# Delta rounds of a two-block model: solve steps one in a slot, spreads in two GpSimd operations, doubling levels four and five moved by five slots

## The reference

```python
k_beta = kc * bc[..., None]
v_beta = vc * bc[..., None]
lower = jnp.where(strict, jnp.einsum('bhnik,bhnjk->bhnij', k_beta, kc) * decay, 0.0)
t_inv = lax.linalg.triangular_solve(eye + lower, eye, left_side=True, lower=True, unit_diagonal=True)
u = t_inv @ v_beta
w = t_inv @ (k_beta * jnp.exp(gc)[..., None])
intra = jnp.where(tril, jnp.einsum('bhnik,bhnjk->bhnij', qc, kc) * decay, 0.0)
def step(state, xs):
    v_new = u_i - w_i @ state
    o_i = qd_i @ state + intra_i @ v_new
    state = state * jnp.exp(gl_i)[..., None, None] + jnp.swapaxes(ks_i, -1, -2) @ v_new
```

## Time and profile before

| | us |
|---|---|
| median of 3 runs | 3521.67 |
| lowest, highest | 3516.02, 3525.56 |
| the profiled execution | 3509.0 |
| its span | 3507.2 |

### The profile page before, as it was taken

The page is one execution under the profiler, slowest core; times in us unless marked ns, Lnnn a source line. Parts: engine busy times, 40 slices in busy tenths (PEclk is TensorE's granted clock), DMA queues, the critical chain, the costliest instruction groups (busy, mean ns, idle before and its releaser), DMA issues.

```text
span 3507.2 us, 51167 instructions
## 1 busy us (share of the span) xinstructions
PE 3350.6 (96%) x22310; PEld 2162.8 (62%) x22310; DVE 1580.3 (45%) x2993; ACT 761.7 (22%) x1580; POOL 379.4 (11%) x298
## 2 busy tenths in 40 slices
PE   8999998999999999999999899998999999899999
PEld 3566666888884657788887454554445656434343
DVE  4454553788743225688832666555212204201011
ACT  2323332211003025311001333233222320211111
POOL 0010110233001000122100211212100001000000
PEclk9999998999999999999999999998999999899999
DMA  5321202255651220156622111100221114699997
GB/s 198 121 74 46 87 7 78 80 180 180 204 157 61 72 77 9 49 156 187 185 84 74 48 37 26 36 25 1 58 66 43 48 44 150 248 421 421 421 421 284
DMA packets 355791, 452.81 MB, mean 129 GB/s; under 512 B 25712, under 2 KB 282992, under 8 KB 331760
## 3 DMA queue, kind: packets, MB, share of 16 engines
q1 hardware_dynamic: 355568, 449.55, 37.4%
HBM read 445.27 MB, written 4.20 MB: 128 GB/s over the span
## 4 chain that ended last, share of the span: by engine, by line
PE 85%; DVE 8%; DMA 3%; ACT 3%; issue 1%; POOL 0%; SPq 0%; POOLq 0%; DVEq 0%; ACTq 0%
PE bank L79 84%; DVE A L70 2%; DVE A L76 2%; DMA A<-in_w_up 2%; ACT A L87 1%; DMA W<-in_w_up 1%; DVE A L73 1%; PE bank L82 0%; POOL A L73 0%; DVE H L70 0%; ACT SM L87 0%; DVE SM L76 0%; DVE X L76 0%; DMA A<-in_x 0%; ACT H L87 0%
## 5 line engine op out<-in xcount | busy, mean ns | idle before, releaser
L79 PE MATMUL bank<-A 64*64 64x64 f32 (+6 forms) x11424 | 1004.2, 271 | 59.9 <-ACT A L87 27.8
L79 PEld LDWEIGHTS bank<-A 64*64 64x64 f32 (+3 forms) x11424 | 785.8, 152 | 322.7 <-issue 117.9
L79 PE MATMUL bank<-A,W 128*128 128x256 f32 (+1 forms) x2240 | 719.0, 475 | 2.9 <-DMA W<-in_rw_g 1.6
L79 PE MATMUL bank<-H,W 128*128 128x512 f32 (+2 forms) x1712 | 644.4, 526 | 24.8 <-ACT H L87 14.4
L79 PEld LDWEIGHTS bank<-A,W 128*128 128x128 f32 x2240 | 417.8, 191 | 253.9 <-issue 213.0
L87 ACT ACTIVATE A<-bank 128x64 f32<-128x64 f32 (+4 forms) x493 | 208.6, 427 | 1434.6 <-PE bank L79 1339.7
L79 PEld LDWEIGHTS bank<-H,W 128*128 128x128 f32 (+1 forms) x1712 | 316.5, 192 | 289.3 <-issue 257.5
L79 PE MATMUL bank<-A,H 128*64 128x512 f32 (+2 forms) x1224 | 309.6, 572 | 6.1 <-DMA A<-in_w_up 3.3
L70 DVE TENSOR_TENSOR A<-bank,A 128x256 f32<-128x256 f32 (+1 forms) x350 | 157.9, 462 | 178.1 <-PE bank L79 158.9
L70 POOL TENSOR_TENSOR A<-A 128x512 f32<-128x512 f32 (+1 forms) x103 | 145.6, 1420 | 749.6 <-ACT A L87 389.6
L87 ACT ACTIVATE A<-A 128x512 f32<-128x512 f32 (+1 forms) x238 | 138.0, 610 | 398.8 <-DVE A L70 368.5
(11 more groups left out here) (185 smaller groups left out, 2576.5 us busy)
## 6 DMA issues: line engine op xcount, KB each, us to landing
A<-in_w_gate SPq DMA_DIRECT2D x47, 1024.0 KB, 22.4
W<-in_mod_w SPq DMA_DIRECT2D x45, 1024.0 KB, 7.3
A<-in_w_up SPq DMA_DIRECT2D x42, 1024.0 KB, 19.3
A<-in_w_down SPq DMA_DIRECT2D x35, 1024.0 KB, 27.0
W<-in_mlp_up SPq DMA_DIRECT2D x64, 512.0 KB, 5.4
W<-in_mlp_down SPq DMA_DIRECT2D x128, 256.0 KB, 4.0
W<-in_w_mod SPq DMA_DIRECT2D x24, 1024.0 KB, 5.4
W<-in_w_up SPq DMA_DIRECT2D x22, 1024.0 KB, 19.0
```

The source lines that it names most:

```text
L79: return self.e.matmul(o, l, r, start=start, stop=stop, skip_group_check=True)
```

## The change

In `dv_dscores` every solve step stands in a slot of its own, 1 to 14 in slots 3 to 16. The spreads of ScalarE and GpSimd stand in slot 17, the two transposes in slot 19. GpSimd's four `tensor_scalar` operations (64 partitions by 256) become two `tensor_tensor` operations (64 partitions by 512) that multiply the solved block, repeated twice, by the mask, repeated. `du` 4 stands in slot 22, `dt`/`dtt` 4 in slot 23, `du` 5 in slot 26, `dtt` 5 in slot 27, and so on with their partners on VectorE and ScalarE. The tokens keep their slots.

```diff
+        def spread16(e, st, x, rows=slice(0, P)):
+
+            n = rows.stop - rows.start
+            mask = C("iota")[rows, 68:70].unsqueeze(1).unsqueeze(3).broadcast_to([n, 16, 2, 16])
+            return e.tt(st.rearrange("p (c q j) -> p c q j", q=2, j=16), x.unsqueeze(2).broadcast_to([n, 16, 2, 16]), mask, MUL)
...
+            yield from idle(12)
+            tokens(0)
+            yield from idle(4)
+            tokens(1)
+            yield from idle(4)
+            tokens(2)
+            yield from idle(2)
+            pe.wait_ge(s_gp, ngp["dm", hd])
+            pe.wait_ge(s_dv, ndv["dt", hd, 3])
+            each(3, m8, DT).then_inc(s_pe, npe("du", hd, 4))
+            yield
+            pe.wait_ge(s_dv, ndv["dtt", hd, 3])
+            pe.wait_ge(s_dv, ndv["da", hd, 4])
+            each(4, TT, DA).then_inc(s_pe, npe("dt", hd, 4))
+            each(3, DA, TT).then_inc(s_pe, npe("dtt", hd, 4))
+            yield
+            tokens(3)
+            yield from idle(2)
+            pe.wait_ge(s_ac, nac["dt", hd, 4])
+            each(4, m8, DT).then_inc(s_pe, npe("du", hd, 5))
+            yield
+            pe.wait_ge(s_dv, ndv["dtt", hd, 4])
+            pe.wait_ge(s_dv, ndv["da", hd, 5])
+            each(4, DA, TT).then_inc(s_pe, npe("dtt", hd, 5))
             yield from idle(5)
...
         def gp_dscores(gp, hd):
...
-            yield from idle(12)
+            yield from idle(15)
             gp.wait_ge(s_dv, ndv["dinv", hd])
-            for n in range(2):
-                for h, i in zip(half, ("p i c -> p i c", "p i c -> p c i")):
-                    gp.wait_ge(s_gp, ngp.n)
-                    m = gp.ts(of16(DAM)[h, :, 16 * n:16 * n + 16], DXI[h, :, :].rearrange(i), parity(n, h), None, MUL, None)
-                    m.then_inc(s_gp, ngp() if n == 0 or h == half[0] else ngp("dett", hd))
+            for h, i in zip(half, ("p i c -> p i c", "p i c -> p c i")):
+                gp.wait_ge(s_gp, ngp.n)
+                m = spread16(gp, DAM[h, :], DXI[h, :, :].rearrange(i), h)
+                m.then_inc(s_gp, ngp() if h == half[0] else ngp("dett", hd))
             gp.wait_ge(s_gp, ngp["dett", hd])
-            yield from idle(18)
+            yield from idle(15)
...
         def ac_dscores(ac, hd):
...
+            for n in range(2):
+                yield from idle(4 if n else 7)
+                ac.wait_ge(s_pe, npe["dtok", hd, n])
...
+            yield
+            ac.wait_ge(s_dv, ndv["dinv", hd])
...
+            yield from idle(6)
+            ac.wait_ge(s_pe, npe["dt", hd, 4])
+            ac.act(DT, bank8(4), COPY).then_inc(s_ac, nac("dt", hd, 4))
+            yield from idle(9)
...
         def dv_dscores(dv, hd):
...
             for j in range(1, 15):
-                if j in (1, 3, 4, 5, 6, 7, 9, 10, 11, 12, 13):
-                    yield
+                yield
                 solve16(dv, DXI, DXTMP, j).then_inc(s_dv, ndv() if j < 14 else ndv("dinv", hd))
-            yield
-            yield
+            yield from idle(3)
             dv.wait_ge(s_ac, nac["det", hd])
             dv.wait_ge(s_gp, ngp["dett", hd])
             dv.e.transpose(by16(DT), of16(TT.rearrange("p c t -> p (c t)"))).then_inc(s_dv, ndv("dt", hd, 3))
...
+            yield
+            tokens(2)
+            yield from idle(2)
+            dv.wait_ge(s_pe, npe["du", hd, 4])
+            dv.wait_ge(s_dv, ndv["dtt", hd, 3])
+            dv.tt(DA, bank8(3), dover8("d_lev4"), MUL).then_inc(s_dv, ndv("da", hd, 4))
+            yield
+            dv.wait_ge(s_pe, npe["dtt", hd, 4])
+            dv.e.tensor_copy(TT, bank8(3)).then_inc(s_dv, ndv("dtt", hd, 4))
+            yield
+            tokens(3)
+            yield from idle(2)
...
```

More of the change, by code:

```diff
@@ L2359, in pe_dscores @@
                 m.then_inc(s_pe, npe("dsb", hd, q))
-            yield from idle(5)
[L2361 to L2369, removed]
-                yield
[L2371 to L2377, removed]
-                yield
-                yield
[L2380 to L2386, removed]
@@ L2387, in pe_dscores, with tokens @@
-            yield from idle(7)
+            def tokens(n):
+                b = 1 + n % 2
+                pe.wait_ge(*left[b])
+                turn(vf if n < 2 else QK[:, :, 0, :], b, n % 2).then_inc(s_pe, npe("dtok", hd, n))
+                left[b] = (s_ac, nac["dtok", hd, n]) if n < 2 else (s_dv, ndv["dtok", hd, n])
+            yield from idle(12)
[5 more added lines that the diff above has]
+            yield from idle(2)
@@ L2408, in ac_dscores @@
                 ac.wait_ge(s_pe, npe["dheaded", hd - 2])
[L2409 to L2425, removed]
-                yield
-            yield from idle(7)
+            for n in range(2):
+                yield from idle(4 if n else 7)
+                ac.wait_ge(s_pe, npe["dtok", hd, n])
+                ac.act(VTs[hd % 2][:, 4 * n:4 * n + 4, :], BK[1 + n][:, :].rearrange("p (s d) -> p s d", s=4), COPY).then_inc(s_ac, nac("dtok", hd, n))
+            yield
+            ac.wait_ge(s_dv, ndv["dinv", hd])
+            for k in range(2):
+                for h, i in zip(half, ("p i c -> p c i", "p i c -> p i c")):
+                    m = ac.act(of16(TTf)[h, :, 16 * k:16 * k + 16], DXI[h, :, :].rearrange(i), COPY, scale=parity(k, h))
+                    m.then_inc(s_ac, nac() if k == 0 or h == half[0] else nac("det", hd))
+            yield from idle(6)
+            ac.wait_ge(s_pe, npe["dt", hd, 4])
+            ac.act(DT, bank8(4), COPY).then_inc(s_ac, nac("dt", hd, 4))
+            yield from idle(9)
         def dv_dscores(dv, hd):
@@ L2484, in dv_dscores, with tokens @@
-            yield from idle(7)
+            def tokens(n):
+                dv.wait_ge(s_pe, npe["dtok", hd, n])
+                q = slice(4 * n - 8, 4 * n - 4)
+                m = dv.tt(KTs[hd % 2][:, q, :], BK[1 + n % 2][:, :].rearrange("p (s d) -> p s d", s=4),
+                          BEK[:, q, hd:hd + 1].broadcast_to([P, 4, 128]), MUL)
+                m.then_inc(s_dv, ndv("dtok", hd, n))
+            yield
+            tokens(2)
+            yield from idle(2)
+            dv.wait_ge(s_pe, npe["du", hd, 4])
@@ L2488, in pe_dchain @@
+            yield
+            dv.wait_ge(s_pe, npe["dtt", hd, 5])
+            dv.e.tensor_copy(TT, bank8(4)).then_inc(s_dv, ndv("dtt", hd, 5))
+            yield from idle(5)
         def pe_dchain(pe, hd):
```

24 lines of the change are left out of this document (3 added, 21 removed).

## The result

| | before | after |
|---|---|---|
| median, 11 executions each (us) | 3521.67 | 3529.3 |
| lowest, highest | 3513.85, 3525.65 | 3523.42, 3535.77 |
| ratio, 95% interval | | 1.0026, 1.0015 to 1.0036 |
| the profiled execution, its span | 3509.0, 3507.2 | 3531.0, 3529.2 |
| mean granted clock | 0.979 | 0.975 |

The account below looks back on a forecast made before the run. TensorE, with 85% of the chain that ended last, was taken as the bound. Terms summed to +8.1 us, 3517 for the profiled execution; adding the median's 12.7 us gave 3530 us (+0.23%), range 3517 to 3543.

Parts of the forecast that it names:

- Doubling levels, +8.8 and +3.8: Rounds 3 to 7: TensorE idles 0.88 us after each du, +8.8 us; U2 copy uncovered in slots 18 and 22, +3.8.
- Slot 4, -2.1: Rounds 4 to 8: solve step 2 leaves slot 3, so the ones-matmul waits 0.42 us less each, -2.1 us.
- Sums ahead, +4.4 and, in round 2, +1.5: GpSimd's sums delay VectorE's solve step: 0.87 us at slot 12 in rounds 3 to 7, +4.4; round 2, +1.5 us.
- Slot 16, -1.3, and slots 16 and 17, -4.5: Rounds 4 to 7: fewer solve steps before slot 16, -1.3 us; PB copy and dx waits go, -3.7, round 3 -0.8.
- The cover of dx, 0: Slot 21: dx ready before TensorE wants du2, with about 0.8 us of cover, so no cost.
- that rival: Cover of dx breaks, GpSimd slower or blocking VectorE: 1 us more in five rounds, +13 us, 3535; chance 0.06.
- Round 2, -1.5: Round 2, no chain: PB copy wait shrinks by ScalarE's spreads and three solve steps, less the sums' cost; -1.5 us.
- Round 8, 0: Round 8: slot 17's du2 spared a wait, doubling costs about 2.5 us; net 0, between -3 and +3.
- Round 9, +0.5: Round 9: one gate matmul per slot covers da and U2; GpSimd's X products run among solve steps; +0.5 us.
- The clock, "even in the sum": Half-clock stretches: slot 12 gains, slots 16 and 17 lose theirs, slot 4 keeps most; taken as even.
- The rival "faster": TensorE's clock never falls in slots 4 and 16, some 12 us: -4 us, or -10 with harmless sums, 3512; chance 0.12.
- the rival "slower through the clock": Slot 12 in rounds 4 to 7 falls to 1.2 GHz, slots 22/23 and 26/27 sometimes: +15 to +25, 3540; chance 0.28.

Follow-up runs that it names:

- e6: Kernel before with only the doubling levels moved to slots 22/23 and 26/27; 3533.66 us, ratio to before 1.0038.
- e8: Kernel before with only GpSimd's xsum moved to slot 13, ahead of the spreads of slot 14; 3521.36 us, ratio to before 1.001.
- e2: Kernel after with GpSimd's xsum and xnormed in slot 17, behind the spreads; 3519.44 us, ratio to before 1.0005.
- e12: Kernel before with only GpSimd's X products (xnormed) moved to slot 13, ahead of the spreads; 3526.61 us, ratio to before 1.0022.
- e3: Kernel after with ScalarE's spreads in slot 18, behind the gate copy; 3522.15 us, ratio to before 1.0014.
- e5: Kernel before with only GpSimd's two spread operations in place of four; 3517.89 us, ratio to before 0.9997.
- e10: Kernel after with doubling levels one slot earlier and ScalarE's gate copy ahead of its spreads; 3506.27 us, ratio to before 0.9965.
- e4: Kernel after with levels one slot earlier, GpSimd's sums and X products behind its spreads, and gate copy ahead of ScalarE's spreads; 3492.74 us, ratio to before 0.9933.
- e7: Kernel before with only solve step 2 moved from slot 3 to slot 4; 3517.02 us, ratio to before 0.9986.
- e9: Kernel after with doubling levels one slot earlier and GpSimd's sums and X products behind the spreads; 3497.16 us, ratio to before 0.9943.
- e11: Kernel with all three corrections (levels, GpSimd's side work, gate copy), but GpSimd's four old spread operations; 3494.22 us, ratio to before 0.9934.
- e1: Kernel after with both doubling levels one slot earlier; 3507.94 us, ratio to before 0.998.

## Why the prediction was right, and where it was not

The time was right (3530 forecast, 3529.3 measured; the stage +8.1 and +8.4). Against the steps:

- **Doubling levels, +8.8 and +3.8**: right, the first a little too large. 0.79 us, not 0.88, twice in each of five rounds is 7.9 us; 0.38 us more before two dds of each round is 3.8. The chain's short waits, set at 0, gave back 0.16 us a round. e6 has +11.8 us of idle time in rounds 3 to 7 for the 12.6. In round 8, where 2.5 us were allowed for the levels, e6 has 3.5.
- **Slot 4, -2.1**: right, 2.25 to 1.79 us in all five rounds.
- **Sums ahead, +4.4 and, in round 2, +1.5**: the mechanism was right, the size too large and the place half right. The wait was to grow at slot 12 alone, to 1.9 us. It grew by 0.43 at slot 10, where U2's copy stands behind ScalarE's late operations for the norms, and by 0.26 at slot 12, to 1.28: 0.69 us a round, not 0.87. In e8, with the solve steps of the kernel before, the two slots cost 0.82. Round 2 cost 1.4 (e8). By the page "SBUF — State Buffer" of the Trainium skill, Who interferes with whom, VectorE with two inputs in SBUF and GpSimd exclude one another, and issue order decides. The traces agree with the first (some 0.43 us became 2.33). Of the second they show one side only: GpSimd's operation had started first, by 0.11 us, and VectorE was the one that waited.
- **Slot 16, -1.3, and slots 16 and 17, -4.5**: the waits went as said, but the second sum was taken from one round. The 0.46 and 0.47 us of round 5 were multiplied by four. In the kernel before rounds 4 and 6 have neither, and round 7 only the first, at 0.41 us. So rounds 4 to 7 had 1.3 us to give, not 3.7, and with round 3's 0.84 it was 2.2. Slot 16 itself waits 0.34 us in every round after, where 0.66 was implied. e2 has the 0.67. The other 0.33 us hang on the clock: in the kernel after TensorE spends 3.4 us at half clock between slots 12 and 16 in each of rounds 4 to 7, so it comes to slot 16 later, and VectorE has caught up. The kernel before shows both cases: 0.98 us in rounds 4 to 6, without such a stretch, and 0.34 in round 7, with one.
- **The cover of dx, 0**: held. No wait stands before slot 21's du2 in rounds 3 to 7, and the transposes wait for ScalarE (3.5 us of 4.8), so that rival falls.
- **Round 2, -1.5**: idle time -1.6, the PB copy is waited for 2.75 us in place of 4.36. The round became 2.9 us shorter, the rest being clock.
- **Round 8, 0**: idle time -0.4, with the levels' 3.5 us in it (e6). Slot 17's du2 is spared its 2.77 us, as was said; slot 21's du2 waits 1.33 instead, and slot 4 waits 0.45 less. The rest isn't taken apart.
- **Round 9, +0.5**: this step failed. Idle time +5.3, half clock +6.9 us, the round 8.5 us longer. That one gate matmul in each slot covers `da` and U2 was wrong for slots 17 and 26, which have none: +0.38 and +0.79 us, and e6 has these +1.2 by themselves. And the step didn't price either queue: the X products were named and put at next to nothing, though the rows of the sums stood beside them (2.61 us in place of 0.77; e2 and e12), and ScalarE's gate copy behind four spreads wasn't seen at all (2.27 us; e3).
- **The clock, "even in the sum"**: failed. The stretches of half clock were to leave slots 16 and 17 and come to slot 12, and they did: behind slot 16 they went from two rounds to none, and behind slot 12 from one round to all four of 4 to 7. But slot 4 was to keep most of its five and kept two, in rounds 6 and 8, and round 2 lost its one. Rounds 2 to 8 spend 27.2 us at half clock, where it was 44.3, which is worth 8.5 us. The rival "faster" had this half right; the rival "slower through the clock" had slot 12 right, each time in rounds 4 to 7; but slots 22/23 and 26/27 have no fall in any of these rounds, and it left out what slots 4 and 16 gave back.

So the exact total owes much to luck. In rounds 2 to 8 the idle time grew by 6.9 us, where the terms gave 7.6 (with errors of either sign in them), but the clock, which wasn't counted, gave all of it back: these rounds take 434 us before and after. The whole 8.4 us of the stage lie in round 9, to which the forecast gave 0.5.

## What to carry to other kernels

When a piece of work moves in a hand-made order, list everything on the same queues that keeps its slot, and say for each whether it now stands ahead or behind; here three such neighbours and one slot made the difference between 1.0026 and 0.9933. A dependent pair of short steps (`du`, then `dt`) needs a slot in which independent work of the same engine lies between them, and that is to be looked for in the slot table before moving it. Taking 18 of 26 us of waiting from an engine off the critical path changed nothing that could be measured. And a wait that is read in one round is not to be multiplied by the number of rounds before it has been looked up in each.

## What the runs showed of the hardware

The length of a wait alone didn't decide whether TensorE fell to 1.2 GHz behind it. Counted is a fall when the granted clock goes to 0.50 within 2.5 us of the start of the ones-matmul of slot 4, in rounds 4 to 8. After waits of 2.23 to 2.25 us that was so in five of five rounds in before, e5 and e12, but in two of five in e6 and e8. After waits of 1.78 to 1.80 us it was so in five of five in e2, in four in e10, in two in after, e4, e7, e9 and e11, and in one in e1 and e3. So the shorter wait was followed by a fall less often, 21 times in 45 against 19 in 25, but didn't rule it out.

The ones-matmul by itself doesn't tell. In round 5 of e6 it runs at full clock (1.12 us, in the rows of e6), and the fall comes 1.0 us behind its start, into four fetch matmuls that take 3.6 us at full clock:

```profile
2180.96 5.29 PE L79 MATMUL bank<-H,W 128*128 128x512 f32 x8
```
```profile
2181.00:2184.40 3.40, 3.40 (x6) 1.33 (x5) 1.96 (x5) 0.00 (x0) 0.00 (x0) 0.50 0.00 0
```

Nor do the order of work and the waits ahead decide it. Rounds 5 and 6 of the kernel after have the same order and, from slot 22 of the round before up to slot 4, the same waits (0.38, 0.79, 0.38, 0.79, 0.38 and 1.79 us). The clock fell behind slot 4 in round 6 and not in round 5. e12, which has before's instruction order until round 9, repeats before's falls: they begin at the same places of rounds 2 to 8 to 0.1 us, and the rounds have the same lengths. But that is one pair of executions, and whether the moment at which a wait begins matters, and this pair happened to agree in it, wasn't tested. For a forecast this means a term of several us (here 5 in the stage) whose sign rows of single waits don't give.
